# Branch B of a hybrid attention step: heads 0 and 1 scored on stacked high and low key halves, heads 2 and 3 as before, three cache copies moved

## The chip, the cores and the metric

One NeuronCore of a Trainium2 chip runs the whole program. The metric is the device time of one execution in microseconds (us); lower is better.

## The reference, cut to what matters

One layer of a decoder trunk on 1024 prompt rows and 8 x 8 sample rows. A projection of the normalised input gives queries, keys and values for four attentions: G = 0 is branch B (4 heads, causal over all 1024 rows, two softmax maps per head), G = 1 to 3 are three dilated windows (branch A). The change is in branch B of the prompt:

```python
# q, k: (b, s, 4 heads, 2 maps, 64), both RMS-normed per 64; v: (b, s, 4, 128)
scores = einsum('bqhcd,bkhcd->bhcqk', q, k) * 64 ** -0.5
scores = scores - slopes[h] * (q_pos - k_pos)            # ALiBi, causal
p = softmax(scores)                                      # one softmax per map c = 0, 1
a = p[:, :, 0] - lam * p[:, :, 1]
o = einsum('bhqk,bkhe->bqhe', a, v)
```

The outputs are the layer's result, the new keys and values, and three updated window buffers of the sample part, most of which are plain copies of the old cache, shifted by 8 rows.

## The kernel before

Everything is float32. The engines' programs are written out by hand, one function per engine, and meet only through semaphores. The order of work is fixed in the source.

- **Projections.** `block_(u)` runs one block of 512 weight columns over 9 row tiles (8 of the prompt, one of the sample). Blocks u = 0, 1, 2 are queries, keys and values of G = 0, then 3 to 5 those of G = 1 and so on. A weight chunk is loaded by SP into one of four places of `raw`, ScalarE rounds it to float32r (`w_hi`), and GpSimd subtracts to get the rest (`w_lo`, `split_lo`, L1071). TensorE forms w_hi x high part, w_lo x high part, w_hi x low part (L2074 to L2076). While block u runs, block u + 1 is loaded and split, one chunk per row tile.
- **Turning queries and keys.** VectorE norms a tile and transposes it in 32x32 pieces, SP stores it in DRAM (`blocks_scr`), and `load_turned` (L781) loads it back so that a head's dimensions lie on the partitions: `qT` and `kT`, [128, 4 x 1024], columns by head. On the 128 partitions lie the two maps of a head, 64 dimensions each. The 16 loads of queries go out in the key block (two per row tile), the 16 of keys in the value block (four in each of the row places 1 to 4).
- **Padding.** A product with K = 128 over both maps would mix them. So GpSimd scales the queries into `qz` [128, 2, 1024], in which map 0 has zeros on the lower 64 partitions and map 1 on the upper (L1125, `scaled`). Head 0 is padded in the value block at place 1 (`pad_first`: two memsets, 16 scalings), the others tile by tile as TensorE frees the place (`pad_queries`).
- **Attention B** (`attention_b` on PE, DVE, ACT). Step e = 0 to 31 is head e // 8 and query tile TILE_ORDER[e % 8] = 7, 0, 6, 1, 5, 2, 4, 3; its scores are 128 to 1024 columns wide. For each map PE scores (L2176, float32) into PSUM, VectorE adds the bias table `tB` and takes the minimum (L1711), ScalarE takes the exponential in place (L1376). VectorE then combines the maps (reciprocal L1721, weight L1723, L1728), PE turns the result in pieces (L2186), ScalarE moves it (L1357), PE multiplies with the values (L2197), and ScalarE stores the scaled output into `qT` (L1362). PE may score one piece ahead of VectorE: `pe.wait_ge(bs, N - 1)`.
- **SP's order at this place.** In the last place of the value block SP waits for all splits of block u = 3 (`sp.wait_ge(lo_done, first_chunk[4])`), because `tB` lies on `raw`, then loads the tables of heads 0 and 1 (L833). Then `tables(0)`: in each head four copies of the cache (`copy_cache`, L718, up to 2 MB each, at most two under way), ahead of heads 2 and 3 the next table. After it `attention_out` stores the outputs.
- **The end.** `out_tile` runs 18 tiles of the output projection; for each, SP stores the result `yo`, loads the residual `xl` for two tiles later, and for the first 7 issues one cache copy. VectorE adds `xl` (L2015), PE has three PSUM banks.

## Time and profile before

| | before |
|---|---|
| median of 3 runs | 1658.04 us (1654.12 to 1663.19) |
| the profiled execution | 1655.49 us, its span 1653.5 us |
| busy: DVE / ACT / POOL | 46% / 34% / 42% |
| granted clock of TensorE over the span | 0.994 |
| DMA: bytes, packets | 369.84 MB, 351487 |

One execution is in the profile. Times count from the start of its span. PE is TensorE's matmuls, PEld its weight loads, DVE VectorE, ACT ScalarE, POOL GpSimd, SP the engine that issues most DMAs (SPq its queue). A group of rows gives count, busy time and mean duration of one; "idle before" says how long the engine waited just ahead of such instructions and for whom. Matmuls overlap, so their rate is read from starts and not from durations.

### The profile page before, as it was taken

What the parts mean: (1) busy time and instruction counts of PE and PEld (TensorE: products, weight loads), DVE (VectorE), ACT (ScalarE), POOL (GpSimd) and SP (SyncE); (2) the same over time, 40 slices, a digit from 0 to 9 for tenths busy, and PEclk for the clock granted to TensorE, in tenths of its full rate; (3) what the DMA queues carried; (4) which work ended last, traced back from release to release, by engine and by line L of the source; (5) the groups of instructions that cost most, each with busy time, mean ns of one, the idle gap of its engine ahead of it and who ended that gap; (6) DMA issues with size and microseconds to landing.
All of it is one profiled execution on the core that took longest, in us unless ns stands there. A gap on an engine that the chain in (4) does not pass through costs nothing.

```text
span 1653.5 us, 37307 instructions
## 1 busy us (share of the span) xinstructions
PE 1597.9 (97%) x14616; PEld 1373.3 (83%) x14616; DVE 757.4 (46%) x1852; ACT 564.2 (34%) x1341; POOL 697.7 (42%) x958
## 2 busy tenths in 40 slices
PE   6999999999999999999999989999999899999999
PEld 5787677878899999999999877778787788888787
DVE  6632577332473332733326545344454433588411
ACT  5321477121362222712126233333343334411300
POOL 5676340466543666446666112222121121665500
PEclk9999999999999999999999999999999999999999
DMA  5358897337982369933797899889988977865593
GB/s 165 111 148 189 270 305 233 101 85 153 262 283 86 90 158 248 321 108 96 172 260 250 304 303 323 280 306 316 325 292 297 332 251 238 290 197 171 196 332 100
DMA packets 351487, 369.84 MB, mean 224 GB/s; under 512 B 164113, under 2 KB 208274, under 8 KB 351314
## 3 DMA queue, kind: packets, MB, share of 16 engines
q1 hardware_dynamic: 306354, 308.55, 61.9%
q10 hardware_dynamic: 44960, 58.92, 10.7%
q8 instruction: 117, 1.92, 0.5%
q14 instruction: 56, 0.46, 0.1%
HBM read 310.83 MB, written 143.85 MB: 275 GB/s over the span
## 4 chain that ended last, share of the span: by engine, by line
PE 84%; DVE 4%; DMA 3%; POOL 3%; issue 2%; ACT 2%; SPq 1%; ACTq 1%; POOLq 0%; DVEq 0%
PE ps L2074 13%; PE ps L2075 13%; PE ps L2076 13%; PE ps L2127 5%; PE ps L2128 5%; PE ps L2129 5%; PE ps L2230 4%; PE ps L2287 4%; PE ps L2176 4%; PE ps L2250 3%; PE ps L2348 3%; PE ps L2237 2%; PE ps L2331 2%; DMA v_in<-in_cache_a_kv 2%; PE ps L2197 2%
## 5 line engine op out<-in xcount | busy, mean ns | idle before, releaser
L1071 POOL TENSOR_TENSOR w_lo<-raw,w_hi 128x512 fp32r<-128x512 f32 x140 | 181.3, 1299 | 400.8 <-ACT w_hi L1281 399.9
L2074 PE MATMUL ps<-w_hi,hT 128*128 128x512 f32 x824 | 333.0, 404 | 2.1 <-POOL hT L1058 1.0
L2075 PE MATMUL ps<-w_lo,hT 128*128 128x512 f32 x824 | 330.1, 401 | 0.0
L2076 PE MATMUL ps<-w_hi,hT 128*128 128x512 f32 x824 | 330.1, 401 | 0.0
L2127 PE MATMUL ps<-w_hi,hT 128*128 128x256 f32 x768 | 225.3, 293 | 4.3 <-issue 3.9
L2074 PEld LDWEIGHTS ps<-w_hi,hT 128*128 128x128 f32 x824 | 206.2, 250 | 22.8 <-issue 1.4
L2076 PEld LDWEIGHTS ps<-w_hi,hT 128*128 128x128 f32 x824 | 206.2, 250 | 20.4
L2075 PEld LDWEIGHTS ps<-w_lo,hT 128*128 128x128 f32 x824 | 206.4, 250 | 19.4
L2129 PE MATMUL ps<-w_hi,hT 128*128 128x256 f32 x768 | 216.8, 282 | 1.0 <-issue 1.0
L2128 PE MATMUL ps<-w_lo,hT 128*128 128x256 f32 x768 | 217.4, 283 | 0.0
L1125 POOL TENSOR_SCALAR qz<-qT,qcol 64x128 f32<-64x128 f32 x256 | 156.0, 609 | 108.6 <-PE ps L2176 54.8
L1281 ACT ACTIVATE w_hi<-raw 128x512 fp32r<-128x512 f32 x158 | 98.7, 628 | 279.2 <-DMA raw<-in_w_in 237.0
L2127 PEld LDWEIGHTS ps<-w_hi,hT 128*128 128x128 f32 x768 | 147.3, 192 | 12.1 <-issue 11.5
L2128 PEld LDWEIGHTS ps<-w_lo,hT 128*128 128x128 f32 x768 | 147.6, 192 | 1.8 <-issue 1.8
L2129 PEld LDWEIGHTS ps<-w_hi,hT 128*128 128x128 f32 x768 | 147.2, 192 | 0.0
L1801 DVE STREAM_TRANSPOSE k_in<-k_in 128x512 f32<-128x512 f32 x224 | 138.5, 678 | 3.9 <-DMA k_in<-in_cache_a_kv 2.6
L1052 POOL TENSOR_TENSOR rs<-ss,half_pow 128x8 f32<-128x8 f32 (+3 forms) x81 | 127.0, 1568 | 6.7
L1673 DVE TENSOR_TENSOR zn<-ps,rs 128x512 f32<-128x512 f32 (+1 forms) x72 | 49.7, 691 | 145.5 <-POOL rs L1052 145.5
L1391 ACT ACTIVATE sA<-sA,st_sum 128x128 f32<-128x128 f32 (+1 forms) x192 | 86.1, 449 | 58.3 <-DVE st_sum L1767 52.4
L1335 ACT ACTIVATE ps<-ps 128x512 f32<-128x512 f32 (+1 forms) x72 | 41.8, 580 | 182.1 <-PE ps L2076 173.6
L1658 DVE TENSOR_REDUCE ss<-ps 128x8 f32<-128x512 f32 (+1 forms) x72 | 49.7, 690 | 117.0 <-ACT ps L1335 116.9
L2230 PE MATMUL ps<-kT,qz 128*128 128x128 f32 (+1 forms) x384 | 100.4, 348 | 1.0 <-issue 0.8
(229 smaller groups left out, 2758.7 us busy)
## 6 DMA issues: line engine op xcount, KB each, us to landing
out<-in_cache_a_kv SPq DMA_DIRECT2D x32, 2040.0 KB, 13.5
k_in<-in_cache_b_kv SPq DMA_DIRECT2D x128, 256.0 KB, 4.4
v_in<-in_cache_b_kv SPq DMA_DIRECT2D x128, 256.0 KB, 6.3
raw<-in_w_in SPq DMA_DIRECT2D x104, 256.0 KB, 3.4
k_in<-in_cache_a_kv SPq DMA_DIRECT2D x104, 256.0 KB, 8.1
v_in<-in_cache_a_kv ACTq DMA_DIRECT2D x96, 256.0 KB, 6.4
out<-in_cache_a_kv SPq DMA_DIRECT2D x8, 2016.0 KB, 10.3
raw<-in_w_in ACTq DMA_DIRECT2D x40, 256.0 KB, 6.8
```

The source lines that it names most:

```text
L1052: return pool.tensor_tensor(out, in_, half_pow[0:r, 0:heads], ALU.pow)
L1071: pool.tensor_tensor(lo, raw_of(q), hi.bitcast(F32), ALU.subtract).then_inc(lo_done, 1)
L1125: return pool.tensor_scalar(qz[rows, half, cols], qT[rows, c * SEQ + i * P:c * SEQ + (i + 1) * P], qcol[rows, (0 if G else 1):(0 if G else ...
L1281: act.activation(weights(q)[0], raw_of(q), ACT.Copy).then_inc(hi_done, 1)
L1801: dve.transpose(k_in[:, gg % NKS, j, :], k_in[:, gg % NKS, j, :]).then_inc(s_kt, 1)
L2074: pe.matmul(z, hi, wh, start=first, stop=False)
L2075: pe.matmul(z, hi, wl, start=False, stop=False)
L2076: return pe.matmul(z, lo, wh, start=False, stop=last)
L2127: pe.matmul(part, hi, wh, start=k == 0, stop=False)
L2128: pe.matmul(part, hi, wl, start=False, stop=False)
L2129: ins = pe.matmul(part, lo, wh, start=False, stop=k == KC - 1)
L2230: pe.matmul(bank(s % 4)[:, 0:W], qz[:, hh, i * P:(i + 1) * P], kT[:, k0:k0 + W], start=True, stop=True).then_inc(aq, 1)
```

## The change

In heads 0 and 1 (HALVED = 2) a map's 64 dimensions fill the 128 partitions twice. `load_head` loads queries and keys of one map into both halves of the partitions. GpSimd makes of the keys `k_hl` (partitions 0 to 63: the keys rounded to float32r, 64 to 127: what is left of them) in `key_parts`, one call for each head and map, and of the queries `q_hi` (rounded) and `q_lo` (the rest) in `query_parts`, one call for each query tile, both maps at once. TensorE then scores each piece by two float32r products, q_hi on k_hl and q_lo on k_hl, accumulated in PSUM; pieces under 256 columns are widened to 256. `k_hl` lies on `kT` and `q_lo` on `qT`, in place; `q_hi` and the scratch `k_hi` on the place of `zn`, `kn` and `qz`.

Heads 2 and 3 keep padded queries and one float32 product. Their 8 key loads and 8 query loads (`load_whole_head`) go out in `tables(0)`, when head 0 and head 1 are biased, and `qz` is cleared tile by tile in head 1. Outputs of head 1 and 2 change places in `qT` (O_AT). In each of the four heads SP issues 3, 2, 4, 4 copies of the cache instead of 4 each, and in the output 10 instead of 7.

```diff
-COPIES_B, COPIES_A = 16, ((2, 2, 2, 2), (2, 2, 2, 1), (1, 1, 1, 1))
-COPIES_V, COPIES_OUT = 2, 7
+COPIES_B, COPIES_A = (3, 2, 4, 4), ((2, 2, 2, 2), (2, 2, 2, 1), (1, 1, 1, 1))
+COPIES_V, COPIES_OUT = 2, 10
...
+        q_hi = place("q_hi", [P, 2, SEQ], F32R, at=[work])
+        q_lo = place("q_lo", [P, NC * SEQ], F32R, at=[q_base])
+        k_hl = place("k_hl", [P, NC * SEQ], F32R, at=[k_base])
+        k_hi = place("k_hi", [P, CW], F32R, at=[work + 4 * 4 * CW])
...
+        SPLIT_0, HALVED = 2 * TILES, 2
+        O_AT, Q_AT = (0, 2, 1, 3), (0, 2, 1, 3)
...
@@ sync
+            def load_head(kind, part):
+                h, rest = divmod(part, 8)
+                mp, d, j = rest // 4, rest // 2 % 2, rest % 2
...
+                src = bass.AP(base.tensor, base.offset + h * P + HD * mp + 32 * j, [[CW, 32], [32 * CW, SEQ // 32], [1, 32]])
+                p0, c0 = HD * d + 32 * j, head_at(h, mp)
+                out = (kT if kind == "k" else qT)[p0:p0 + 32, c0:c0 + SEQ]
...
+                        if h == 2:
+                            sp.wait_ge(kt_in, 256)
+                            for k in range(HALVED, B_HEADS):
+                                load_whole_head("k", k)
+                        if h >= 2:
+                            sp.wait_ge(qt_in, 256 + 64 * (h - 2))
+                            load_whole_head("q", h)
+                        more_copies(COPIES_B[h])
...
@@ gpsimd, block_
-                    if kind == "v" and at_ == 1:
+                    if kind == "v" and at_ == 1 and G:
                         pad_first(G)
+                    if kind == "v" and 0 < at_ < 5 and G == 0:
...
+                        for n in range(2 * at_ - 2, 2 * at_):
+                            query_parts(n)
+                    if kind == "v" and 4 < at_ < NT and G == 0:
+                        key_parts(0, at_ - 5) if at_ < 7 else key_parts(1, 0)
...
+            def query_parts(e):
+
+                h, i = e // 8, TILE_ORDER[e % 8]
+                if h:
+                    pool.wait_ge(bq, 16 + 2 * (e - 8) + 2)
...
+                pool.tensor_scalar(hi_q, raw_q, qcol[:, 1:2], None, ALU.mult)
+                link(pool.tensor_scalar(raw_q, raw_q, qcol[:, 1:2], None, ALU.mult))
+                pool.tensor_tensor(lo_q, raw_q, hi_q.bitcast(F32), ALU.subtract).then_inc(qz_ready, 1)
+
+            def key_parts(h, mp):
+
+                pool.wait_ge(kt_in, 256)
+                pool.wait_ge(*lo_ready(last_split[0]))
+                pool.wait_ge(qz_ready, 8)
+                for x0 in range(head_at(h, mp), head_at(h, mp) + SEQ, CW):
+                    cols = slice(x0, x0 + CW)
+                    link(pool.tensor_copy(k_hi[HD:P, :], kT[HD:P, cols]))
+                    link(pool.tensor_tensor(k_hl[HD:P, cols], kT[HD:P, cols], k_hi[HD:P, :].bitcast(F32), ALU.subtract))
+                whole = slice(head_at(h, mp), head_at(h, mp) + SEQ)
+                pool.tensor_copy(k_hl[0:HD, whole], kT[0:HD, whole]).then_inc(h_lo, 1)
+                pool.wait_ge(h_lo, SPLIT_0 + 2 * h + mp + 1)
...
@@ gpsimd, pad_queries
+                key_parts(1, 1)
+                for e in range(8, 16):
+                    query_parts(e)
+                for c in range(HALVED, B_HEADS):
...
@@ tensor, scores
+                    if e % 8 == 0 and h < HALVED:
+                        pe.wait_ge(h_lo, SPLIT_0 + 2 * h + mp + 1)
+                    if e == 8 * HALVED and mp == 0:
+                        pe.wait_ge(kt_in, 384)
                     pe.wait_ge(bs, N - 1)
                     for w0 in range(0, W, CW):
+                        if h < HALVED:
+                            w, k0 = min(CW, max(2 * P, W - w0)), head_at(h, mp)
+                            z, keys = ps[:, mp * 1024 + w0:mp * 1024 + w0 + w], k_hl[:, k0 + w0:k0 + w0 + w]
+                            pe.matmul(z, q_hi[:, mp, s * P:(s + 1) * P], keys, start=True, stop=False)
+                            ins = pe.matmul(z, q_lo[:, k0 + s * P:k0 + (s + 1) * P], keys, start=False, stop=True)
+                            continue
```

GpSimd's order in the value block, from the first weight split of block u = 3 on. `w_lo` is the split of a weight chunk, `qz` the padded queries. Before:

```order
L1071 TENSOR_TENSOR w_lo_74<-raw,w_hi_73 128x512 [waits hi_done]
L1135 MEMSET qz 64x1024 [waits k_out0,k_out1,blocks_out0,k_out2,blocks_out1,blocks_turned]
L1136 MEMSET qz 64x1024 [waits pool_step]
L1125 TENSOR_SCALAR qz<-qT,qcol 64x128 [waits qT_in,setup,pool_step]
L1125 TENSOR_SCALAR qz<-qT,qcol 64x128 x15
L1071 TENSOR_TENSOR w_lo_74<-raw,w_hi_73 128x512 [waits hi_done,qz_ready]
L1071 TENSOR_TENSOR w_lo_74<-raw,w_hi_73 128x512 [waits hi_done] x6
```

After, further down in the same block: the last of eight query tiles, then the keys of head 0, map 0 (`key_parts`), and the next split. Line numbers are of the changed kernel.

```order
L1191 TENSOR_SCALAR q_hi<-qT,qcol 128x2x128
L1192 TENSOR_SCALAR qT<-qT,qcol 128x2x128
L1193 TENSOR_TENSOR q_lo<-qT,q_hi 128x2x128 [waits pool_step]
L1117 TENSOR_TENSOR w_lo_74<-raw,w_hi_73 128x512 [waits hi_done]
L1202 CAST k_hi<-kT 64x512 [waits qz_ready,lo_done,kT_in]
L1203 TENSOR_TENSOR k_hl<-kT,k_hi 64x512 [waits pool_step]
L1202 CAST k_hi<-kT 64x512 [waits pool_step]
L1203 TENSOR_TENSOR k_hl<-kT,k_hi 64x512 [waits pool_step]
L1205 CAST k_hl<-kT 64x1024 [waits pool_step]
L1117 TENSOR_TENSOR w_lo_74<-raw,w_hi_73 128x512 [waits hi_done,h_lo]
L1202 CAST k_hi<-kT 64x512 [waits qz_ready,lo_done,kT_in]
```

Ahead of this piece stand the first split and seven more triples of L1191, L1192, L1193 with three splits between them; behind it come the other two calls of `key_parts` in this block, each with a split after it. Where two memsets and 16 scalings stood before six of the splits, there now stand 24 instructions on queries and 15 on keys among the seven splits that follow the first.

SP's order from the last places of the value block on (`tables(0)`). `tB` is the bias table, `out<-in_cache_a_kv` a copy of the cache. Before:

```order
L833 DMA tB<-in_bias_b 128x1024 [waits lo_done]
L833 DMA tB<-in_bias_b 128x1024
L823 DMA out<-v_sb 128x512 [waits v_ready]
L718 DMA out<-in_cache_a_kv 16x15x512 [waits const_in]
L718 DMA out<-in_cache_a_kv 16x63x512
L718 DMA out<-in_cache_a_kv 16x48x680 [waits copies]
L718 DMA out<-in_cache_a_kv 16x48x680 [waits const_in]
L718 DMA out<-in_cache_a_kv 16x48x680 [waits copies]
L718 DMA out<-in_cache_a_kv 16x48x680 [waits const_in]
L718 DMA out<-in_cache_a_kv 16x15x512 [waits copies]
L718 DMA out<-in_cache_a_kv 16x63x512 [waits const_in]
L833 DMA tB<-in_bias_b 128x1024 [waits b_biased]
```

After:

```order
L871 DMA tB<-in_bias_b 128x1024 [waits lo_done]
L871 DMA tB<-in_bias_b 128x1024
L861 DMA out<-v_sb 128x512 [waits v_ready]
L733 DMA out<-in_cache_a_kv 16x15x512 [waits const_in]
L733 DMA out<-in_cache_a_kv 16x63x512
L733 DMA out<-in_cache_a_kv 16x48x680 [waits copies]
L733 DMA out<-in_cache_a_kv 16x48x680 [waits const_in]
L733 DMA out<-in_cache_a_kv 16x48x680 [waits copies]
L871 DMA tB<-in_bias_b 128x1024 [waits b_biased]
L804 DMA kT<-blocks_scr0k 32x32x32 [waits kT_in]
L804 DMA kT<-blocks_scr0k 32x32x32 x7
L804 DMA qT<-blocks_scr0q 32x32x32 [waits qT_in]
```

The table loads wait for the same splits as before. The loads of keys and queries for heads 2 and 3 stand behind the third table and ahead of the copies of head 2.

## Rows read from the trace of the kernel before

**Rows 1.** The page: busy time, share of the span and instructions of each engine.

```profile
PE 1597.9 (97%) x14616; PEld 1373.3 (83%) x14616; DVE 757.4 (46%) x1852; ACT 564.2 (34%) x1341; POOL 697.7 (42%) x958
```

**Rows 2.** Busy time by stretch (PE, PEld, DVE, ACT, POOL, clock, DMA share, GB/s).

```profile
203.00:230.00 27.00, 27.00 (x156) 19.97 (x155) 20.77 (x56) 19.32 (x53) 10.22 (x16) 1.00 0.90 302
```

**Rows 3.** Timeline of VectorE in attention B (start us, us): first biasing of heads.

```profile
177.76 1.23 DVE L1711 CUSTOM_DVE_ANT_0 sB<-ps,tB 128x1024 f32<-128x1024 f32 x1 [1.58 <-PE ps L2176]
...
203.41 1.22 DVE L1711 CUSTOM_DVE_ANT_0 sB<-ps,tB 128x1024 f32<-128x1024 f32 x1 [1.11 <-issue]
...
258.39 1.22 DVE L1711 CUSTOM_DVE_ANT_0 sB<-ps,tB 128x1024 f32<-128x1024 f32 x1 [1.11 <-issue]
```

**Rows 4.** Timeline of TensorE: projection products, then scores.

```profile
170.15 0.40 PE L2076 MATMUL ps<-w_hi,hT 128*128 128x512 f32 x1
170.39 0.39 PE L2074 MATMUL ps<-w_hi,hT 128*128 128x512 f32 x1
...
204.33 1.88 PE L2176 MATMUL ps<-kT,qz 128*128 128x512 f32 x4
```

**Rows 5.** Scores by source line, and VectorE by line, 175.5 to 286 us.

```profile
L2176 PE MATMUL ps<-kT,qz x192: 272/540/697, 175.7 to 283.4; 128*128 128x512 f32 x96, 128*128 128x128 f32 x32, 128*128 128x384 f32 x32, 128*128 128x256 f32 x32
...
L1711 DVE CUSTOM_DVE_ANT_0 sB<-ps,tB 128x1024 f32<-128x1024 f32 (+7 forms) x64 | 47.1, 755 | 16.6 <-PE ps L2176 13.1 <-issue 3.3
...
L1721 DVE RECIPROCAL rlB<-st_sum 128x2 f32<-128x2 f32 x32 | 5.2, 162 | 8.7 <-ACT sB L1376 8.7
```

**Rows 6.** Timeline of GpSimd in the value block.

```profile
142.88 0.95 POOL L1135 MEMSET qz<- 64x1024 f32 x1
143.88 0.95 POOL L1136 MEMSET qz<- 64x1024 f32 x1
144.94 10.85 POOL L1125 TENSOR_SCALAR qz<-qT,qcol 64x128 f32<-64x128 f32 x16
...
169.04 1.30 POOL L1071 TENSOR_TENSOR w_lo<-raw,w_hi 128x512 fp32r<-128x512 f32 x1 [1.29 <-ACT w_hi L1281]
```

**Rows 7.** Timeline of the SP queue; landing times of tB.

```profile
139.78 4.29 SPq L781 DMA_DIRECT2D kT<-blocks_scr0k  x4
...
170.99 0.93 SPq L833 DMA_DIRECT2D tB<-in_bias_b  x2
...
DMA to landing us min/median/max: 3.8/7.0/14.3
```

**Rows 8.** Timeline of VectorE and GpSimd ahead of the output.

```profile
1475.70 0.69 DVE L1848 TENSOR_TENSOR ogA<-ogA 128x512 f32<-128x512 f32 x1
...
1479.06 2.99 POOL L1215 TENSOR_TENSOR sig<-sig,sig 128x512 f32<-128x512 f32 x2
...
1479.12 1.77 DVE L1860 TENSOR_TENSOR ogB<-ogB,rs 128x512 f32<-128x512 f32 x1 [1.41 <-POOL rs L1052]
```

**Rows 9.** GpSimd by line and form (count, busy us, mean ns).

```profile
L1071 POOL TENSOR_TENSOR w_lo<-raw,w_hi 128x512 fp32r<-128x512 f32 x140 | 181.3, 1299 | 400.8 <-ACT w_hi L1281 399.9
L1125 POOL TENSOR_SCALAR qz<-qT,qcol 64x128 f32<-64x128 f32 x256 | 156.0, 609 | 108.6 <-PE ps L2176 54.8
...
L1179 POOL COPY q_rep<-qTs 32x64 f32<-32x64 f32 x128 | 29.5, 230 | 27.4 <-issue 10.9 <-PE ps L2292 10.8
L1179 POOL COPY q_rep<-qTs 32x32 f32<-32x32 f32 x128 | 26.1, 204 | 17.6 <-PE ps L2287 11.8
...
L1058 POOL TENSOR_TENSOR hTs<-hn,hTs 128x256 fp32r<-128x256 f32 x2 | 1.5, 732 | 2.2 <-ACT hTs L1268 2.2
```

**Rows 10.** Busy time by stretch, and TensorE at the start of the output.

```profile
1545.00:1560.00 15.00, 11.96 (x47) 8.63 (x46) 6.79 (x11) 6.89 (x13) 9.41 (x8) 0.83 0.62 196
...
1557.17 0.63 PE L2074 MATMUL ps<-w,hT 128*128 128x512 f32 x1
```

**Rows 11.** Timeline of VectorE in the output.

```profile
1613.29 0.68 DVE L2015 TENSOR_TENSOR yo<-ps,xl 64x512 f32<-64x512 f32 x1 [5.53 <-DMA xl<-in_x_sample]
...
1622.20 0.69 DVE L2015 TENSOR_TENSOR yo<-ps,xl 128x512 f32<-128x512 f32 x1 [3.50 <-PE ps L2076]
```

More of the change, by code:

```diff
@@ L605, in stored, with head_at, turned_in_dram @@
             return 16 * (NC + (NC + NT) * G)
+        def head_at(h, mp):
+            return (2 * h + mp) * SEQ
+        def turned_in_dram(G):
+            return 384 + 256 * G if G else 256
         def part_of(big, small, part, i):
@@ L769, in store_blocks, with load_whole_head @@
                     .then_inc(blocks_sent(G, kind, i)[0], 16)
+            def load_head(kind, part):
+                h, rest = divmod(part, 8)
+                mp, d, j = rest // 4, rest // 2 % 2, rest % 2
+                if part == 0:
+                    for i in range(NT - 2, NT):
+                        sp.wait_ge(*blocks_sent(0, kind, i))
+                base = blocks_scr[0][kind == "k"][0:1, 0:1]
+                src = bass.AP(base.tensor, base.offset + h * P + HD * mp + 32 * j, [[CW, 32], [32 * CW, SEQ // 32], [1, 32]])
+                p0, c0 = HD * d + 32 * j, head_at(h, mp)
+                out = (kT if kind == "k" else qT)[p0:p0 + 32, c0:c0 + SEQ]
+                sp.dma_start(out.rearrange("p (b r) -> p b r", r=32), src).then_inc(kt_in if kind == "k" else qt_in, 16)
+            def load_whole_head(kind, h):
+                base = blocks_scr[0][kind == "k"][0:1, 0:1]
+                c0 = (h - HALVED if kind == "k" else Q_AT[h]) * SEQ
+                for j in range(4):
+                    src = bass.AP(base.tensor, base.offset + h * P + 32 * j, [[CW, 32], [32 * CW, SEQ // 32], [1, 32]])
+                    out = (kT if kind == "k" else qT)[32 * j:32 * j + 32, c0:c0 + SEQ]
+                    sp.dma_start(out.rearrange("p (b r) -> p b r", r=32), src).then_inc(kt_in if kind == "k" else qt_in, 16)
             def load_turned(G, kind, part):
+                if G == 0:
+                    load_head(kind, part)
+                    return
                 c, j = divmod(part, 4)
@@ L868, in attention_out @@
                     sp.wait_ge(*((ao, 8 + 32 * (G - 1) + 8 * (c + 1)) if G else (bo, 8 + 8 * (c + 1))))
+                    at_ = (c if G else O_AT[c]) * SEQ
                     sp.dma_start(tiles_of(o_scr[G], G)[c],
-                                 qT[:, c * SEQ:(c + 1) * SEQ].rearrange("p (i e) -> p i e", i=NT))\
+                                 qT[:, at_:at_ + SEQ].rearrange("p (i e) -> p i e", i=NT))\
                         .then_inc(o_out, 16)
@@ L1134, in pad_first @@
                     pool.wait_ge(k_out[s], k_sent[s][TILES * G + NT])
+            def pad_first(G):
+                zn_left(G)
                 link(pool.memset(qz[0:HD, 1, :], 0.0))
                 link(pool.memset(qz[HD:P, 0, :], 0.0))
-                pool.wait_ge(setup, 1)
-                pool.wait_ge(qt_in, 256 * (G + 1))
-                for i in range(NT) if G else TILE_ORDER:
+                pool.wait_ge(qt_in, turned_in_dram(G))
+                for i in range(NT):
                     scaled(G, 0, i, 0)
@@ L1153, in pad_queries @@
                     return
-                for c in range(1, NC):
+                key_parts(1, 1)
+                for e in range(8, 16):
+                    query_parts(e)
+                for c in range(HALVED, B_HEADS):
+                    pool.wait_ge(qz_ready, 8 * c)
+                    pool.wait_ge(qt_in, 256 + 64 * (c - 1))
                     for s, i in enumerate(TILE_ORDER):
                         pool.wait_ge(bq, 16 + 16 * (c - 1) + 2 * s + 2)
-                        scaled(G, 0, i, c)
-                        scaled(G, 1, i, c).then_inc(qz_ready, 1)
+                        if c == HALVED:
+                            link(pool.memset(qz[0:HD, 1, i * P:(i + 1) * P], 0.0))
+                            link(pool.memset(qz[HD:P, 0, i * P:(i + 1) * P], 0.0))
+                        scaled(G, 0, i, Q_AT[c])
+                        scaled(G, 1, i, Q_AT[c]).then_inc(qz_ready, 1)
             for G in range(4):
```

17 lines of the change are left out of this document (12 added, 5 removed).

## The prediction

> **What bounds the kernel now.** I read the page first: TensorE is busy for 97% of the span [rows 1], so what PE does counts, and so does every wait that holds PE. Then the table of busy time by stretch for the attention of branch B [rows 2]: PE is busy for 27.0 of 27 us, but VectorE for 20.8 and ScalarE for 19.3 of the same 27, so no more than some 6 us per head can be cut from PE before another engine ends last. The heads follow each other by the start of VectorE's first biasing of 1024 columns: 177.76 (head 0), 203.41 (head 1), 258.39 us (head 3) [rows 3]. That is 25.65 us for head 0 and 27.49 for a later one. Last I read GpSimd and SP ahead of that stage [rows 6, 7], because the change puts its new work there.
>
> **The scores.** Four records of a 128x512 product of plain float32 take 1.88 us, the last of them 0.59, so they start 0.43 us apart [rows 4]. A product has two such records: the 96 of that shape are 48 products [rows 5]. A product on rounded halves (w_lo, hT) starts 0.235 us after its neighbour (170.15, 170.39) [rows 4]. A head scores 2 x 128 x (1+...+8) = 9216 columns. Now that is 18432 columns of records at 0.43/512, 15.5 us. After, the narrow pieces are widened to 256 (512 columns more in a head) and each is done twice: 19456 columns at 0.235/512, 8.9 us. TensorE saves 6.6 us in head 0 and in head 1, nothing in 2 and 3.
>
> How much of it reaches the end is set by VectorE. Over four heads it waits 13.1 us for the scores and 8.7 us for ScalarE [rows 5]. Only the first kind can go. A head then lasts its 20.8 us of busy time, 2.2 for ScalarE, and about 1.2 for semaphores and leftovers: 24.2. Head 1 gains 27.5 - 24.2 = 3.3 us (bounds: 2, and the full 6.6).
>
> **What else meets VectorE in head 0.** GpSimd is busy 10.2 of 27 us in a head now [rows 2]. After the change it has the last key split and eight query splits to do while head 0 is scored, some 5 + 8 x 2.4 = 24 us, so it is nearly always busy. A VectorE product of two SBUF tensors, 128x512, takes 0.69 us alone and 1.77 us beside a GpSimd instruction that started just before it [rows 8]. In a head, VectorE issues 16 instructions with two SBUF inputs (L1723, L1728). If half of them wait about half a microsecond, that is 4 us. Head 0 then lasts 20.8 + 2.2 + 4 = 27.0 and a little, where 25.65 was: +1.5 us (bounds: -3 without any meeting, +10 if each waits a whole instruction). I take a value below the middle because scores gate GpSimd too, so it must pause. The Trainium skill, page "SBUF — State Buffer", section "Who interferes with whom", states that a VectorE instruction with two SBUF inputs contends with a GpSimd one that reads SBUF, and that whichever came first holds the shared ports for its whole length. By that rule the sum would go to the upper bound as long as GpSimd never pauses; the 1.77 us row agrees with it.
>
> **The start of the stage: the largest term.** VectorE can't bias until its table tB is loaded, and SP loads that only after GpSimd's last weight split for the next block, because tB lies on the staging buffer raw. Today that split starts at 169.04 and takes 1.30 [rows 6], the tables are issued at 170.99 and land after 3.8 at best [rows 7]. PE ends the values only at 175.7 [rows 5], so all of it is covered. GpSimd starts its query work at 142.88 and has two memsets and 10.85 us of scalings there [rows 6]. After the change these are its instructions between 142.9 and the end of the last split:
> - 16 scalings of 128x256. A 64x128 one takes 0.609; 128 elements more cost 0.10 us by the slope of the copies (204 to 230 ns for 32 to 64 elements) or 0.28 by that of the subtractions (732 to 1299 ns for 256 to 512) [rows 9]. I take 0.80, between the two; bounds 0.60 (length free) and 1.21 (twice). 12.8 us.
> - 8 subtractions of 128x256 at 0.73: 5.8. 6 of 64x512 at 1.30, as one of 128 partitions: 7.8. 7 weight splits at 1.30: 9.1 [rows 9].
> - 6 casts of 64x512 and 3 of 64x1024. No cast is in the trace. By the copies' slope [rows 9] 0.59 and 1.01, and a memset of 1024 is 0.95 [rows 6]: 6.5 us. If a cast costs what a subtraction does, 1.30 and 2.4: 15.0. I take the first, a cast having one input like a copy.
> - 23 waits on its own last instruction, 0.05 each (142.88 + 0.95 to 143.88 [rows 6]): 1.2.
>
> The sum is 43.2 us, so the last split ends at 186.1, the first table is issued within 0.3 and lands 3.8 later, and VectorE starts at 190.2 instead of 177.8: **+12.4 us** (bounds +9.2 and +27.5). The first key half is ready near 173, so PE scores the first map in time and the second near 180. Then it sits for some 10 us, because it may run only one piece ahead of VectorE. Behind the same wait on SP is the first cache copy, which is not needed. The Trainium skill, "GPSIMD Engine Reference", section "Performance versus the Vector engine", gives about 1.03 cycles for an element of a one-input body. An estimate by that page puts a 256 scaling at 0.71 and the term at +11.0. The copies and the memset here agree with it; no row shows it for a scaling.
>
> **TensorE's clock.** After a stall the granted clock is lower: between 1545 and 1560 us PE was busy for 11.96 of 15, the clock was 0.83 over that stretch, and a record of 128x512 lasted 0.63 us instead of 0.40 [rows 4, 10]. Head 0 will start at the lower of the two levels (1.2 GHz), but there are no values to compute yet and VectorE is behind: +0.5 (0 to 3).
>
> **Loads and copies.** The 16 transposing loads of queries and the 16 of keys stay where they are, now for two heads, each in two places. Sixteen more (8 for keys, 8 for queries) go out in heads 1 and 2. Four such take 4.29 us to issue [rows 7], so the twelve ahead of head 2 take some 13. SP gets to them when head 0 is biased, near 217, and head 2 starts near 241, so I cost them at nothing; head 1 hides them. Without that cover they would cost those 13 us. Three of 16 copies go to the output. There xl is already late: VectorE waited 5.53 us for it and started at 1613.29, and was on PE's pace again at 1622.20 [rows 11]. PE has three banks, so it needed the one of 1613.29 when it began the tile that ends at 1622.2, 5.6 us earlier at 1616.6: 2.6 us were left. Three copies more prolong this by some 20 us: +0.5 (0 to 3).
>
> **The sum.** +12.4 (start) +1.5 (head 0) -3.3 (head 1) +0.5 (clock) +0.5 (output) = +11.6 us on the profiled execution's 1655.49: 1667.1. The median of the three runs, 1658.04, lies 2.55 above that execution, so I forecast 1669.6, **1670 us**.
>
> **Rivals.**
> 1. *The full gain.* Place: heads 0 and 1. VectorE's other waits turn out to be PE's doing as well, and GpSimd is never met. Then each of the two loses PE's 6.6: -13.2 + 12.4 + 1 = +0.2, so 1658: not slower. For: PE is full in these stretches, and VectorE's busy 20.8 just fits into 27.5 - 6.6 = 20.9 [rows 2]. Against: its 8.7 us behind ScalarE. It decides once both heads are under 22 us. Chance 0.22.
> 2. *GpSimd locks VectorE out.* Place: head 0. Sixteen waits of 0.8 us, 12.8 in place of 4: 1679. For: the 1.77 us row. Against: GpSimd's pauses. It decides when the combining instructions of head 0 last twice as long. The rule on the shared ports would give this time. 0.12.
> 3. *A cast costs what a subtraction does.* Place: the key splits ahead of the stage. +8.4: 1678. For: GpSimd's steeper slope where it does arithmetic [rows 9]. Against: its copies. 0.13.
> 4. *The change does not do what it says*: PE isn't spared, since loading other weights for every product costs what the pass saved. No gain in head 1: +3.3, 1673. Against: in the values' products every one has weights of its own and they start 0.235 us apart [rows 4]. 0.05.
>
> **How the numbers follow.** The forecast, a late start and a small gain, has 0.43, the rivals 0.22, 0.12, 0.13 and 0.05, and 0.05 is left for a gain that I don't see, since the cheapest start with the full gain (9.2 - 13.2) is only -4. A measurement of this kernel tells 0.5%, 8.3 us, from no change: slower begins at 1666.3. The forecast gives slower with 0.8 of its chance and same with 0.2. Slower: 0.34 + 0.12 + 0.13 + 0.05 = 0.64. Same: 0.09 + 0.22 = 0.31. Faster: 0.05. The low end of the range is the cheap start with a clean head 0 and the gain taken for head 1 (9.2 - 3 - 3.3 + 1: 1662), moved to 1659 to reach rival 1 halfway; the high end is rivals 2 and 3 together (1670 + 8.8 + 8.4, 1687) and the clock's bound in part, 1688.
>
> **What would show it.** Right: the last weight split ahead of the attention ends near 186 us, VectorE's first biasing is near 190, PE idles some 10 us before it at a lower granted clock after, heads 0 and 1 are 27 and 24 us long, and the stage ends some 10 us later. Wrong: a first biasing before 182, or heads 0 and 1 both under 22 us, or a PE that waits for keys at head 2 or for xl in the output.

## The result and the profile after

The changed kernel takes 1669.91 us (median of 9 runs, 1661.72 to 1676.14), the kernel before on the same chip 1661.15 (9 runs, 1653.21 to 1664.24). The ratio is 1.0064, with a 95% interval of 1.0038 to 1.0090: slower by 10.6 us (6.3 to 15.0). The forecast of 1670 us was met, its range of 1659 to 1688 too. That it was met to a tenth of a microsecond is luck: the forecast was added onto a median of 1658.04 for the kernel before, and that kernel's median was 3.1 us higher when both were timed side by side. The profiled execution took 1674.07 us, span 1672.0; the one of before took 1655.49, span 1653.5. The two profiles are thus 18.5 us apart, more than the timed runs: the one of after lies 4.2 above its median, the one of before 5.7 below. So every stage is counted below from a mark of its own.

The page of the changed kernel, busy time by engine (as [rows 1]):

```profile
PE 1594.2 (95%) x14616; PEld 1375.7 (82%) x14616; DVE 757.7 (45%) x1852; ACT 563.4 (34%) x1341; POOL 742.1 (44%) x1008
```

PE is busy 3.7 us less, GpSimd 44.4 us more.

VectorE's timeline, the first biasing of heads 0 to 3 (as [rows 3]):

```profile
194.57 1.23 DVE L1802 CUSTOM_DVE_ANT_0 sB<-ps,tB 128x1024 f32<-128x1024 f32 x1 [16.35 <-DMA tB<-in_bias_b]
...
218.45 1.22 DVE L1802 CUSTOM_DVE_ANT_0 sB<-ps,tB 128x1024 f32<-128x1024 f32 x1
...
242.30 1.22 DVE L1802 CUSTOM_DVE_ANT_0 sB<-ps,tB 128x1024 f32<-128x1024 f32 x1
...
269.80 1.22 DVE L1802 CUSTOM_DVE_ANT_0 sB<-ps,tB 128x1024 f32<-128x1024 f32 x1 [1.11 <-issue]
```

The first biasing is 16.8 us later than before (14.9 of it in this stage, see the table below), and VectorE stood for 16.35 us waiting for its table. Then heads 0 and 1 take 23.88 and 23.85 us (25.65 and 27.49 before), head 2 27.50.

GpSimd in that stretch by form (142 to 190.6 us: count, busy us, mean ns, as [rows 9]):

```profile
L1117 POOL TENSOR_TENSOR w_lo<-raw,w_hi 128x512 fp32r<-128x512 f32 x8 | 10.3, 1284 | 6.5 <-ACT w_hi L1372 6.3
L1203 POOL TENSOR_TENSOR k_hl<-kT,k_hi 64x512 fp32r<-64x512 f32 x6 | 7.6, 1272 | 0.5
L1191 POOL TENSOR_SCALAR q_hi<-qT,qcol 128x256 fp32r<-128x256 f32 x8 | 7.4, 927 | 0.0
L1192 POOL TENSOR_SCALAR qT<-qT,qcol 128x256 f32<-128x256 f32 x8 | 7.4, 926 | 0.0
L1193 POOL TENSOR_TENSOR q_lo<-qT,q_hi 128x256 fp32r<-128x256 f32 x8 | 5.9, 738 | 0.7
L1202 POOL CAST k_hi<-kT 64x512 fp32r<-64x512 f32 x6 | 3.6, 608 | 0.6
L1205 POOL CAST k_hl<-kT 64x1024 fp32r<-64x1024 f32 x3 | 3.1, 1031 | 0.2
```

The last weight split starts at 189.29 and takes 1.26; SP follows at once (its queue, as [rows 7]):

```profile
190.58 0.81 SPq L871 DMA_DIRECT2D tB<-in_bias_b  x2
...
191.91 20.64 SPq L733 DMA_DIRECT2D out<-in_cache_a_kv  x5
...
218.95 12.19 SPq L804 DMA_DIRECT2D kT<-blocks_scr0k  x8
231.19 3.42 SPq L804 DMA_DIRECT2D qT<-blocks_scr0q  x4
```

TensorE's timeline at the start of the scores (as [rows 4]):

```profile
178.48 0.40 PE L2274 MATMUL ps<-k_hl,q_lo 128*128 128x512 f32 x1
182.79 0.77 PE L2273 MATMUL ps<-k_hl,q_hi 128*128 128x512 f32 x1 [3.92 <-issue]
183.36 0.63 PE L2274 MATMUL ps<-k_hl,q_lo 128*128 128x512 f32 x1
...
195.95 0.55 PE L2273 MATMUL ps<-k_hl,q_hi 128*128 128x256 f32 x1 [11.12 <-DVE st_sum L1802]
...
205.02 0.63 PE L2274 MATMUL ps<-k_hl,q_lo 128*128 128x512 f32 x1
```

PE scores both maps ahead of time and then stands still for 11.12 us. It is at the lower level of its clock (0.63 us for a record that took 0.40) from the second map on, after a pause of 3.92 us, and until past 205. Over 194.57 to 206 the granted clock is 0.50, from 209 on 1.00.

Busy time by stretch, head 1 and head 0 of the changed kernel (as [rows 2]):

```profile
218.45:242.30 23.85, 22.20 (x151) 19.13 (x150) 20.27 (x58) 19.56 (x52) 5.14 (x11) 1.00 0.99 228
194.57:218.45 23.88, 20.94 (x115) 18.18 (x115) 20.25 (x52) 16.21 (x41) 22.36 (x25) 0.75 1.02 332
```

PE has 1.7 us to spare in head 1 and 2.9 in head 0, at a granted clock of 0.75. GpSimd is busy for 22.4 of head 0's 23.9 us. VectorE's busy time looks the same as in head 1, but the two stretches do not hold the same work: head 0 has 52 instructions and head 1 has 58, because the last pair of maps of each head is combined after the next head's first biasing. That one combination takes 1.1 us (0.16 + 0.22 + 0.75), so VectorE worked about 1.1 us longer in head 0 for the same instructions. Its 14 combining instructions there (L1814, L1819) took 1.0 us more than the same ones in head 1.

What VectorE waited for in head 1, before and after (us in total, times, longest):

```profile
DVE sB L1711 <- PE ps L2176: 3.1, 7, 0.7
DVE rlB L1721 <- ACT sB L1376: 2.0, 2, 1.1
```

```profile
DVE rlB L1812 <- ACT sB L1467: 2.9, 4, 1.1
```

The waits for PE are gone. The waits for ScalarE grew by 0.9 us.

The waits of the output stage (us in total, times, longest):

```profile
DVE yo L2106 <- DMA xl<-in_x_prompt: 29.9, 7, 7.4
DVE yo L2106 <- DMA xl<-in_x_sample: 11.0, 2, 6.8
```

Before, these were 17.6 us in 5 waits, now 40.9 in 9. And PE, which never waited for VectorE there before, now waits for VectorE to empty its PSUM banks:

```profile
PE ps L2165 <- DVE yo L2106: 2.9, 2, 2.2
```

All runs follow in one table. Marks: *s* is the start of the first split of the value block's weights (141.65 us before, 143.58 after; the work up to it is the same in every kernel), *start* the first biasing less s, *end* VectorE's first reduction of the next block less s, *output* from the second output tile to the last. Times in us from one profile each, the ratio from timed runs (x4 and y1 were run once and have none).

| kernel | start | head 0 | head 1 | end | output | ratio (95%) |
|---|---|---|---|---|---|---|
| before | 36.1 | 25.7 | 27.5 | 154.4 | 85.9 | 1 |
| changed | 51.0 | 23.9 | 23.9 | 163.9 | 89.6 | 1.0064 (1.0038 to 1.0090) |
| x1 copies back | 51.0 | 23.9 | 42.3 | 185.3 | 85.9 | 1.0166 (1.0135 to 1.0198) |
| x2 copies alone | 36.4 | 25.7 | 27.5 | 154.7 | 88.1 | 1.0016 (0.9992 to 1.0039) |
| x3 table early | 37.5 | 28.4 | 34.2 | 166.2 | 88.8 | 1.0095 (1.0059 to 1.0131) |
| x4 one product | 50.8 | 23.7 | 24.3 | 164.7 | 89.1 | |
| y1 filler | 51.0 | 24.5 | 25.0 | 165.5 | 87.9 | |
| z2 table early, loads free | 37.6 | 28.4 | 24.7 | 156.6 | 88.5 | 1.0028 (1.0009 to 1.0047) |
| z3 loads free only | 51.0 | 23.9 | 23.9 | 164.7 | 87.6 | 1.0062 (1.0038 to 1.0086) |
| y4 fewer at output | 50.9 | 24.1 | 24.2 | 164.4 | 85.9 | 1.0064 (1.0042 to 1.0087) |
| y2 keys on VectorE | 36.2 | 25.8 | 24.0 | 152.5 | 86.6 | 1.0005 (0.9983 to 1.0027) |
| z1 second deal | 36.2 | 25.8 | 24.0 | 151.1 | 85.9 | 1.0020 (1.0002 to 1.0038) |
| w1 third deal | 36.2 | 25.8 | 24.0 | 151.1 | 85.9 | 1.0014 (0.9991 to 1.0037) |

For the change itself: start +14.9, head 0 -1.8, head 1 -3.6, which is the 9.5 us by which the stage ends later, and output +3.7. The remaining 5.3 of the 18.5 us between the two profiles lie where the kernels do the same: +1.9 before the mark s and +4.2 in the stage of the sample rows, less 0.8 elsewhere. That stage, from the weight load that SP issues at 767.77 us in before (779.72 in after) to the first output tile, took between 783.7 and 798.4 us in the profiles of kernels that all do the same there, so a few microseconds of one profile say nothing about it.

### The profile page after: what moved, and what is told of

Same layout as the page of the kernel before. It is cut to its first block, busy times and chain, and to the rows that moved or that the text cites. A ratio compares the mean times of both kernels' runs of the same rounds, so it can differ in the third digit from the quotient of the medians.

```text
span 1672.0 us, 37382 instructions
## 1 busy us (share of the span) xinstructions
PE 1594.2 (95%) x14616; PEld 1375.7 (82%) x14616; DVE 757.7 (45%) x1852; ACT 563.4 (34%) x1341; POOL 742.1 (44%) x1008
## 4 chain that ended last, share of the span: by engine, by line
PE 68%; DMA 8%; DVE 4%; POOL 3%; issue 2%; ACT 2%; SPq 1%; ACTq 1%; DVEq 0%; POOLq 0%
PE ps L2165 10%; PE ps L2166 10%; PE ps L2167 10%; PE ps L2218 4%; PE ps L2331 4%; PE ps L2219 4%; PE ps L2220 4%; PE ps L2389 4%; PE ps L2351 3%; PE ps L2450 3%; DMA v_in<-in_cache_a_kv 2%; DMA xl<-in_x_prompt 2%; PE ps L2338 2%; PE ps L2277 2%; PE ps L2433 2%
## 5 line engine op out<-in xcount | busy, mean ns | idle before, releaser
L1180 POOL TENSOR_SCALAR qz<-qT,qcol 64x128 f32<-64x128 f32 x224 | 137.3, 613 | 65.9 <-PE ps L2331 39.1
```

Source lines behind the costliest of these rows:

```text
L1180: return pool.tensor_scalar(qz[rows, half, cols], qT[rows, c * SEQ + i * P:c * SEQ + (i + 1) * P], qcol[rows, (0 if G else 1):(0 if G else ...
```

## The experiments

**x1: the copies back where they were.** The changed kernel with

```
-COPIES_B, COPIES_A = (3, 2, 4, 4), ...
-COPIES_V, COPIES_OUT = 2, 10
+COPIES_B, COPIES_A = (4, 4, 4, 4), ...
+COPIES_V, COPIES_OUT = 2, 7
```

> The changed kernel with the copies of the kernel before: four in each head of branch B and 7 in the output. Theory (the three moved copies cost the output some 3 to 4 us, but give the loads for heads 2 and 3 their place): from the second to the last addition in the output 86 us instead of 89.6, and SP reaches the key loads of head 2 only some 35 us after the first biasing instead of 24, so that head 2 starts late by 5 to 10 us. Over all 2 to 6 us slower than the changed kernel. Rival (the loads are hidden in any case): head 2 in time, the output shorter, over all 3 to 4 us faster than the changed kernel.

Ratio 1.0166. SP's queue and VectorE's first biasing of head 2:

```profile
189.58 41.16 SPq L733 DMA_DIRECT2D out<-in_cache_a_kv  x8
...
231.49 13.73 SPq L804 DMA_DIRECT2D kT<-blocks_scr0k  x8
245.26 3.67 SPq L804 DMA_DIRECT2D qT<-blocks_scr0q  x4
```

```profile
258.42 1.22 DVE L1802 CUSTOM_DVE_ANT_0 sB<-ps,tB 128x1024 f32<-128x1024 f32 x1 [18.50 <-issue]
```

Eight copies, of which only two may be under way at a time, hold SP for 41 us behind a table that is already 15 us late, and the loads for head 2 queue behind them. So the move of three copies is no side matter: without it the change would cost another 17 us (1.0166 against 1.0064). The theory had the direction and missed the size, 2 to 6 us; its rival is out. The output stage falls back to 85.9.

**x2: the copies alone.** The kernel before with `(3, 2, 4, 4)` and `10` for `16` and `7`.

> The kernel before, with nothing but the copies of the changed one (3, 2, 4, 4 in the heads, 10 in the output). Theory: branch B of this kernel is bound by TensorE, so its heads stay at 25.6 and 27.5 us; in the output VectorE waits for xl some 40 us in sum instead of 17.6 and PE loses 3 to 4 us: 0.2% slower than before. Rival (the late xl in the changed kernel was an accident of its run): within 1 us of before.

Heads unchanged; output +2.2 us, with 44.5 us of waits for xl in 10; ratio 1.0016, an interval that holds both 0 and +6 us, so the cost in the whole is not shown. At the output three copies more cost this profile some 2 us. In the profiles of all the kernels with ten copies there the stage took 86.6 to 89.6 us, in the four with seven 85.9 each: 0.7 to 3.7 us, more than the 0.5 of the forecast.

**x3: the table earlier.** SP issues the first table two splits before the last one; the second still waits for the last, so its region of raw is safe:

```
-sp.wait_ge(lo_done, first_chunk[4])
+sp.wait_ge(lo_done, first_chunk[4] - 2)
 table_b(0)
+sp.wait_ge(lo_done, first_chunk[4])
 table_b(1)
```

> The changed kernel, but SP loads the bias table of head 0 when the first six of the eight splits are done, since that table lies on the first two places of raw alone; the second table waits as before. Theory (the start is late only because the table waits behind GpSimd's splits and key parts): the first biasing at 182 to 185 us instead of 194.6, then held by the second key half, and the stage ends 9 to 12 us earlier; over all 9 to 12 us faster than the changed kernel, within 3 us of the kernel before. Rival (GpSimd's queries and keys of heads 0 and 1 are themselves late): the first biasing early, but a stall of about the same length later in heads 0 or 1, over all under 4 us faster than the changed kernel.

The start came back (179.06 us), and nothing of it reached the end: the stage ended 2.3 us later than in the changed kernel. The theory (9 to 12 us faster) was wrong and its rival, a stall of that length later on, right. VectorE in heads 0 to 2, GpSimd beside it, and SP's queue:

```profile
179.06 1.23 DVE L1803 CUSTOM_DVE_ANT_0 sB<-ps,tB 128x1024 f32<-128x1024 f32 x1 [2.95 <-DMA tB<-in_bias_b]
182.84 1.23 DVE L1803 CUSTOM_DVE_ANT_0 sB<-ps,tB 128x1024 f32<-128x1024 f32 x1 [2.55 <-PE ps L2275]
...
186.18 2.12 DVE L1820 SCALAR_TENSOR_TENSOR sB<-sB,wB 128x1024 f32<-128x1024 f32 x1
...
190.31 1.45 DVE L1820 SCALAR_TENSOR_TENSOR sB<-sB,wB 128x128 f32<-128x128 f32 x1
...
207.48 1.22 DVE L1803 CUSTOM_DVE_ANT_0 sB<-ps,tB 128x1024 f32<-128x1024 f32 x1
...
241.64 1.23 DVE L1803 CUSTOM_DVE_ANT_0 sB<-ps,tB 128x1024 f32<-128x1024 f32 x1 [9.55 <-issue]
```

```profile
186.19 1.03 POOL L1206 CAST k_hl<-kT 64x1024 fp32r<-64x1024 f32 x1
187.30 2.13 POOL L1118 TENSOR_TENSOR w_lo<-raw,w_hi 128x512 fp32r<-128x512 f32 x1
...
190.34 1.27 POOL L1204 TENSOR_TENSOR k_hl<-kT,k_hi 64x512 fp32r<-64x512 f32 x1
...
235.84 0.20 POOL L1248 MEMSET qz<- 64x128 f32 x1 [17.07 <-issue]
```

```profile
190.31 20.60 SPq L733 DMA_DIRECT2D out<-in_cache_a_kv  x5
...
211.63 16.98 SPq L804 DMA_DIRECT2D kT<-blocks_scr0k  x8
228.65 3.69 SPq L804 DMA_DIRECT2D qT<-blocks_scr0q  x4
```

Head 0 takes 28.4 us: VectorE waits 2.55 for the second map's keys, which GpSimd has not split yet, and combines in 2.12 and 1.45 us what takes 1.28 and 0.35 in head 1 of the changed kernel. The first of the two begins together with a cast, which has one input; the weight split that came into it did not hold it but was itself held, to 2.13 us. The second begins together with a subtraction, which has two. Head 1 takes 34.2, because the loads for head 2 come behind five copies. GpSimd had no queries of head 2 until 235.84 and waited 17 us. In the changed kernel it had them at 237.60, after a wait of 18.05 us: the early table moved this by less than 2 us.

**x4: one product in place of two.** The product with q_lo is left out, so the scores lose the low half of the queries:

```
-pe.matmul(z, q_hi[...], keys, start=True, stop=False)
-ins = pe.matmul(z, q_lo[...], keys, start=False, stop=True)
+ins = pe.matmul(z, q_hi[...], keys, start=True, stop=True)
```

> The changed kernel without the second product (q_lo) in heads 0 and 1; their scores lack that part. TensorE saves another 4.4 us in each. Theory (VectorE sets the pace of these heads): heads 0 and 1 stay at 23.9 us within 0.4. Rival (TensorE still does): they fall by 2 us or more, to under 22.

Its busy time by stretch, head 0 and head 1:

```profile
192.37:216.04 23.67, 16.98 (x92) 13.07 (x93) 20.18 (x54) 16.21 (x41) 22.92 (x25) 0.81 1.01 329
216.04:240.38 24.34, 21.27 (x130) 17.53 (x130) 20.36 (x57) 19.56 (x52) 4.69 (x10) 0.93 0.93 224
```

With PE relieved by another 4 us in head 0 (16.98 for 20.94) the head is 0.2 us shorter, and head 1 is not shorter at all, at a granted clock of 0.93. The pace of these heads is VectorE's, with its own 20.3 us and what it waits for others: in head 1 here 3.0 us for ScalarE and 0.4 for PE.

**y1: more GpSimd work in head 0.** Behind each query tile one more scaling of 128x512 into the scratch tile k_hi:

```
+pool.tensor_scalar(k_hi[:, :], hT[0][:, 0, 0:CW].bitcast(F32), qcol[:, 1:2], None, ALU.mult)
```

> The changed kernel with one more GpSimd scaling of 128x512 behind each of the eight query tiles that GpSimd prepares while VectorE works on head 0. The result is written to a scratch tile that is overwritten anyway. It adds about 8 x 1.5 = 12 us of GpSimd work to head 0. Theory A (one-input work of GpSimd does not slow VectorE's steps): head 0 stays at 23.9 us, within 0.5, as long as the key halves of head 1's second map are in time. Rival (any GpSimd work costs VectorE time): head 0 takes 27 us or more.

```profile
191.78:216.25 24.47, 20.58 (x115) 17.65 (x115) 20.76 (x52) 16.20 (x41) 23.89 (x23) 0.80 1.02 332
216.25:241.20 24.95, 22.06 (x148) 19.09 (x149) 21.36 (x58) 19.57 (x53) 18.79 (x25) 1.00 1.12 235
```

That is head 0 and head 1. Only 5 of the 8 scalings (1.56 us each) fell into head 0, since GpSimd had no room for more: it is busy 23.9 of 24.5 us. VectorE is busy 0.5 us longer there than in the changed kernel, and 1.1 us longer in head 1, where the other three fell. The two heads together take 1.7 us more, and the stage ends 1.6 us later. So 12.5 us of added one-input work cost 1.6 us: little, but not nothing. The theory (head 0 at 23.9 us within 0.5) was just missed, the rival (27 us or more) is out. It is paid where an instruction of GpSimd begins just ahead of a combining one. The four combining instructions with one of the added scalings begun 0.07 to 0.14 us ahead took 0.35 to 0.41 us longer (1.63 for 1.28, 0.88 for 0.48, 1.29 for 0.88, 1.56 for 1.15); those with one begun 0.77 us ahead or more took no longer.

**z2 and z3: the two waits apart.** z2 is x3 with two copies instead of five ahead of head 2's loads; z3 is the changed kernel with the same copies and the table still late. y3 is z2's kernel, run once: its first stage has the times of z2 within 1 us.

```
-COPIES_B, COPIES_A = (3, 2, 4, 4), ((2, 2, 2, 2), ...
+COPIES_B, COPIES_A = (1, 1, 4, 4), ((3, 3, 3, 2), ...
```

> The run with the early table once more, with only two copies ahead of head 2's loads instead of five (the other three in the next block's stage). Theory A (head 1 took 34.2 us there because the loads came late behind the copies): head 2's start moves from 241.6 to about 234 us, head 1 takes 25 to 27 us. Rival (GpSimd, with its queries for head 1, is what made head 1 long): head 1 stays over 32 us.

> The kernel of the earlier look with the early table and two copies ahead of head 2's loads, now timed. From its one trace (first biasing 178.5, heads 28.5, 24.7 and 27.5 us, next block 11 us earlier than in the changed kernel) the whole should be at 1659 us or 1.002 of before. Rival (one good profile, not the kernel): over 1.005.

> The changed kernel with only the copies moved as in the run with the early table and free loads (two ahead of head 2's loads, three more in the next block's stage), the table still behind the last split. Theory A (each of the two waits hides the other: with a late table the loads are just in time anyway): no change against the changed kernel, 1.006 of before, head 2 not earlier than 240 us. Rival (the copies alone were the cost): 1.002 or less.

SP's queue in z2, ahead of head 2:

```profile
189.87 1.42 SPq L733 DMA_DIRECT2D out<-in_cache_a_kv  x2
...
207.54 7.64 SPq L804 DMA_DIRECT2D kT<-blocks_scr0k  x8
215.23 4.99 SPq L804 DMA_DIRECT2D qT<-blocks_scr0q  x4
```

The loads go out 4 us earlier than in x3, and the eight of the keys take 7.6 us to issue instead of 17.0. Head 1 falls from 34.2 to 24.7, the stage ends 9.6 us earlier, and the ratio from 1.0095 to 1.0028. Freeing the loads without the table (z3) gives nothing: 1.0062. Nor does the early table without free loads (x3). Only both together give back most of the late start (the stage ends 7.3 us earlier than in the changed kernel, still 2.2 later than before): the two waits hid each other.

**y4: the three copies taken from the output** and given to the next block's stage, `((3, 3, 3, 2), ...` and `7`.

> The changed kernel with the three added copies of the output stage taken back out and given to the next block's stage, one for each of its first three quarters. Theory A (the copies at the output hold up the tiles that are read there): the output stage from the second tile to the last goes from 89.6 back to 86.5 us or less, and the whole is 2 to 3 us faster than the changed kernel, 1.004 to 1.006 of before. Rival (the next block's stage pays the same, or the difference of the output stage was another thing): the whole stays at 1.0064 of before.

The output stage fell by the 3.7 us (89.6 to 85.9), but the ratio stayed at 1.0064. With an interval of 3.7 us on either side this is neither the gain nor its absence. The rival, that the next block's stage pays the same, is not seen in the profile: from that block's first reduction to the weight load ahead of the sample rows it took 471.9 us, in the changed kernel 472.3.

**y2, z1, w1: a kernel with the start at its old place.** The first table is early as in x3; the key halves of head 0 are made by VectorE, which is mostly idle there (a copy of 0.69 us in every 5.6), behind its copies of value tiles 6 and 7; the copies are dealt out as (1, 1, 4, 4) ahead of and between the heads, (3, 3, 3, 2) in the next block.

```
+if G == 0 and at_ in (6, 7):
+    key_parts(at_ - 6)
...
+def key_parts(mp):
+    dve.wait_ge(kt_in, 256)
+    dve.wait_ge(qz_ready, 1)
```

> The changed kernel with three edits together: the first bias table is issued two splits earlier; the key halves of head 0 are made on VectorE, behind its copies of the value block's tiles 6 and 7, and no longer on GpSimd; and of the five copies ahead of head 2's loads only two stay, the others go to the next block's stage (3, 3, 3, 2). Theory A (a late table and the copies ahead of the loads are what costs, and GpSimd's two-input work is what made heads 0 and 1 long in the run with the early table alone): first biasing near 175 us, heads 0 and 1 at 25 to 28 us each, head 2 without a gap, its start near 229 (before: 230.9, changed: 242.3), the whole 2 to 8 us faster than before. Rival B (GpSimd's work that is left collides with heads 0 and 1 as in the earlier run, 28 and 34 us): the stage ends where the changed kernel's does, no faster than before.

The start is that of before, head 0 25.8 us (GpSimd still splits the keys of head 1 beside it), head 1 24.0. The stage ends 1.8 us ahead of before's, and the whole is level with it: 1.0005, where the theory had 2 to 8 us faster. Head 2 took 28.9, probably since the queries of head 3 were loaded behind four copies: in z1, with two there, it took 27.5.

> The run with the key halves of head 0 on VectorE once more (start of the scoring at before's place, heads 0 and 1 at 25.8 and 24.0 us), with the copies dealt out again: two instead of four ahead of head 3's query load, which came 1.4 us late there, and seven instead of ten at the output, the rest in the stages of the two blocks that follow. Theory A: head 2 goes from 28.9 to 27.5 us, the output stage from the second tile on from 86.6 to 86 us, and the whole ends at 3 to 4 us below before (0.998), which five rounds may just tell from before. Rival (copies cost as much where they now stand): within 1 us of before.

z1 has two copies there, `(1, 1, 2, 6)`, `(3, 3, 3, 1)` in the third block and 7 at the output. Its first stage ends 3.3 us ahead of before's, but the third block's took 6.6 us more (133.3 for 126.6, between the weight loads issued at 641.16 and 767.77 us in before). The ratio is 1.0020, slower than before and not 3 to 4 us faster, as the theory had it. The queue of SP there:

```profile
686.58 17.26 SPq L733 DMA_DIRECT2D out<-in_cache_a_kv  x4
703.89 13.49 SPq L916 DMA_DIRECT2D o_scr<-qT  x4
...
722.57 0.91 SPq L755 DMA_DIRECT2D raw<-in_w_in  x2
```

Before, the weights of that last row were issued at 711.03: three copies more, and the next block's first weights are 11.5 us late.

> The kernel with the key halves of head 0 on VectorE, with the copies dealt out a third time. The first new deal lost its gain in the stage of the third block, where eight weight pieces of the last group were issued 11.6 us later behind three more copies (first one at 722.6 against 711.0 us) and the step to the next block took 133.3 instead of 126.6 us. Here that stage has its seven copies back; eight stand behind head 3's query load, eleven in the second block's stage, eight at the output. Theory A: the third stage takes 126.6 us again, the first stage ends 3 us ahead of before's, and the whole is 2 to 4 us faster than before (0.998). Rival (eight copies behind head 3's loads make the next block's weights late, as three did there): the step from the last scoring to the next block is over 1 us longer, and the whole is at 1.000 or above.

w1 has `(1, 1, 2, 8)`, the third block's old seven, and 8 at the output. The third block's step is 126.8 us again, and up to there the kernel is 3.6 us ahead of before (a weight load at 764.18 against 767.77). The whole is not: 1.0014, and 0.998 had been expected. In its profile the sample stage took 792.4 us, 6.6 more than in before's; but x4, whose stage is the same, took 798.4. Whether the 3.6 us are lost in this kernel or in the spread of its runs (the interval is 3.8 us to either side) stays open. None of the three is shown to be faster than before.

## Why the prediction was right

**What bounds the stage.** Confirmed by x4: PE's saving can't be taken further than VectorE's pace. Rival 1 (the full gain, both heads under 22 us) is out, and so is rival 4 (PE is not spared): head 1 gained, and VectorE no longer waits for PE in it.

**The start, +12.4 forecast, +14.9 measured.** The mechanism was right and so were nearly all prices. Subtractions, casts and splits were put at 29.2 us together and took 29.2 (5.9 + 7.6 + 3.6 + 3.1 + seven of the splits, 9.0). The casts took 0.61 and 1.03 for 0.59 and 1.01, which rules out rival 3. The 16 scalings took 0.93, not 0.80: 14.8 us for 12.8; the waits between the instructions made up the other 0.5. A scaling of 128 elements takes 0.61 (on 64 partitions), one of 256 0.93, one of 512 1.56, so it grows by 2.5 ns an element, nearly as a subtraction does (2.2 by [rows 9]) and not as a copy. The estimate by the Trainium skill, page "GPSIMD Engine Reference", section "Performance versus the Vector engine", was 0.71 (with the 1.2 GHz that the page gives for GpSimd it comes to 0.72); the rows disagree for this form, while the casts grow by 0.8 ns an element. The table was issued at once and landed 4.0 us later (3.8 forecast).

**Head 0, +1.5 forecast, -1.8 measured.** This is the step that failed. I had 20.8 us of VectorE's own work, 2.2 for ScalarE and 4 for combining instructions that a nearly always busy GpSimd holds up, 27.0 in all. GpSimd was as busy as I had said (22.4 of 23.9 us), and it did hold up half of them: 8 of 14 took 0.06 to 0.19 us longer than the same ones in head 1. But that is 1.0 us in all, not 4; half a microsecond for each was wrong. The other terms: VectorE's own work in this stretch is 19.2 us and not 20.8, since one combination fewer falls into it (1.1) and since even a later head of the kernel before has 0.5 us more (20.77 against 20.27). The waits for ScalarE were 3.0 us and not 2.2, and 0.6 is left over.

Why so little? Take all combining instructions of heads 0 and 1 in the profiles of the changed kernel and ten of its variants. 98 of them took at least 0.04 us longer than undisturbed. In each of these VectorE got through at a fixed time after the start of the GpSimd instruction ahead of it; it was held for what was left of that time. Those that began later than that were not held, nor were those that began just before the GpSimd instruction.

| GpSimd instruction | its length | VectorE held until (us after its start) | cases |
|---|---|---|---|
| scaling 64x128 | 0.61 | 0.16 | 2 |
| scaling 128x256 | 0.93 | 0.25 to 0.28 | 46 |
| scaling 128x512 | 1.56 | 0.48 to 0.49 | 4 |
| cast 64x512 | 0.61 | 0.40 to 0.41 | 5 |
| cast 64x1024 | 1.03 | 0.82 to 0.83 | 7 |
| subtraction 128x256 | 0.73 | 0.52 to 0.55 | 24 |
| subtraction 64x512 | 1.27 | 1.06 to 1.09 | 10 |

So the casts and the subtractions hold VectorE for most of their length, with one input or with two, and the scalings for under a third of theirs. y2 shows a cast beside a combining instruction that takes 0.35 us undisturbed:

```profile
187.08 1.19 DVE L1834 SCALAR_TENSOR_TENSOR sB<-sB,wB 128x128 f32<-128x128 f32 x1
```

```profile
187.09 1.03 POOL L1204 CAST k_hl<-kT 64x1024 fp32r<-64x1024 f32 x1
```

In the changed kernel the casts and the subtractions of the keys were over before VectorE's first combination in head 0, and what was left beside it were scalings and subtractions of 128x256. With the keys beside the first tiles, as in x3, the same instructions took 3.2 us longer in sum. So the forecast of 4 would have been nearly right for a start in time, and it failed for the late one that it had itself forecast. The Trainium skill, page "SBUF — State Buffer", section "Who interferes with whom", lets a VectorE instruction with two SBUF inputs contend with any GpSimd instruction that reads SBUF, and calls the shared ports an exclusive lock; the whole length for whoever comes first it states for VectorE's two-port mode. The traces agree on the contention, and for casts and subtractions nearly on the length (0.83 of 1.03, 1.08 of 1.27). For scalings they do not (0.27 of 0.93, 0.49 of 1.56). Why they hold VectorE so briefly is open. Rival 2 (16 waits of 0.8 us) is out.

**Head 1, -3.3 forecast, -3.6 measured** (24.2 us forecast, 23.9 measured). The parts were 20.8 + 2.2 + 1.2 and came out as 20.3 of work, 2.9 for ScalarE and 0.7 of the rest. **The clock**, +0.5: the lower level lasted into the middle of head 0, but VectorE's pace ruled: behind the first biasing it waited 0.2 us for PE in head 0. It costs nothing that could be seen.

**Loads and copies.** The loads were costed at nothing, and head 2 started in time, with SP issuing from 218.95, as forecast (217); the twelve took 15.6 us to issue for the 13 forecast. But the cover was thin: GpSimd got head 2's first queries at 237.60, and VectorE began on head 2 at 242.30. In x1 it was gone and cost 18.5 us, with three more copies, where I had put 13 us for it. In x3 it was gone from the other side, once the table was early, and cost 9.55 us. The forecast saw the wait and not that it was the next in line: behind a late start, the stage had a second bound nearly as late. **The output**, +0.5 (bound 3): +3.7 in the changed kernel's profile, outside the bound, and +2.2 with the copies alone. Five loads of xl were late before, nine are now. I had taken the three copies to prolong a lateness that costs little; they also made it deeper, with single waits of up to 7.4 us where 5.5 was the longest. One of the prediction's own signs of being wrong, a PE that waits for xl in the output, came about, by way of VectorE and the PSUM banks (2.9 us).

The sum of the terms, +11.6, came out as +13.2 in the profiles (+9.5 for the stage, +3.7 for the output), and the timed runs give +10.6 (6.3 to 15.0). The errors of the terms were +2.5 at the start, -3.3 in head 0, -0.3 in head 1, -0.5 for the clock and +3.2 at the output. The two large ones in the stage nearly cancelled: the total was better than its parts, and that is luck.

## What to carry to other kernels

Work saved on the busiest engine is worth only what the second engine leaves (here 3.6 of 6.6 us), and preparing it costs the full time on the third one, if a load waits behind that engine. Before moving such a load forward, ask what is next in its queue: here the early table and the free loads gave nothing alone and 6 us together. A long copy in a queue is paid by whatever is issued behind it, in the next stage too (z1). And before comparing an engine's busy time in two stretches, compare the counts: equal times here hid one combination fewer.

## What the runs showed of the hardware

Eight transposing loads took 17.0 us to issue right behind five copies of up to 2 MB in x3 and 7.6 behind two that had long landed in z2; right behind eight copies in x1 they took 13.7, in the changed kernel, 6 us after the last of five, 12.2. What sets this within that range is open. A GpSimd that is busy for 98% of a stretch (y1, head 0) made the combining instructions of VectorE, which have two SBUF inputs, 1.5 us longer in sum. Each is held until a fixed time after the start of the GpSimd instruction ahead of it, and by the table above that time grows by 2.1 ns for each element of a subtraction and by 0.8 to 0.9 ns for each of a cast or of a scaling, though a scaling itself takes 2.5 ns longer for each element.
